# The first norm's weight row: spread by a broadcast transfer, or by TensorE into PSUM

## The reference, cut to what matters

```python
def _rmsnorm(x, g):
    y = x * lax.rsqrt(jnp.mean(x * x, axis=-1, keepdims=True) + NORM_EPS)
    return y * g

h = _rmsnorm(x, lw['g_pre_mix'])      # g_pre_mix: 1024 numbers, one for each column
z = h @ lw['w_in']                    # 1024 x 3488, column groups for the branches
```

## Time and profile before

| what | us |
| --- | --- |
| three executions | 906.77, 908.28, 906.37 |
| median | 906.77 |
| the profiled execution, its own time | 906.51 |
| its span (first to last instruction) | 904.7 |
| TensorE busy in the span | 884.0 |
| VectorE, ScalarE, GpSimd busy | 485.6, 389.0, 75.8 |

### The profile page before, as it was taken

The page is one execution under the profiler, slowest core; times in us unless marked ns, Lnnn a source line. Parts: engine busy times, 40 slices in busy tenths (PEclk is TensorE's granted clock), DMA queues, the critical chain, the costliest instruction groups (busy, mean ns, idle before and its releaser), DMA issues.

```text
span 904.7 us, 13767 instructions
## 1 busy us (share of the span) xinstructions
PE 884.0 (98%) x5501; PEld 802.5 (89%) x5501; DVE 485.6 (54%) x745; ACT 389.0 (43%) x772; POOL 75.8 (8%) x73
## 2 busy tenths in 40 slices
PE   8999999999999988999999999999999999999997
PEld 7888999999976767998789999999999998888885
DVE  5522533334354455564679877777777774343124
ACT  5211422344453565452666454544454443332112
POOL 0300297230030000000000000000000000000000
PEclk9999999999999999999999999999999999999999
DMA  7623245253230001654512333322233326222202
GB/s 270 183 72 91 77 129 169 70 145 104 86 70 1 2 1 40 200 181 175 198 71 70 93 94 95 93 78 78 80 93 94 93 83 242 72 74 90 70 23 117
DMA packets 101455, 91.97 MB, mean 102 GB/s; under 512 B 8480, under 2 KB 85296, under 8 KB 101248
## 3 DMA queue, kind: packets, MB, share of 16 engines
q1 hardware_dynamic: 95216, 86.45, 30.7%
q10 hardware_dynamic: 5280, 2.72, 1.1%
q0 software_dynamic: 896, 1.92, 0.7%
HBM read 79.60 MB, written 12.40 MB: 102 GB/s over the span
## 4 chain that ended last, share of the span: by engine, by line
PE 90%; DVE 5%; ACT 3%; DMA 1%; issue 1%; SPq 0%; ACTq 0%; DVEq 0%
PE ps L1153 26%; PE ps L1155 26%; PE ps L1154 26%; PE ps L1333 2%; PE ps L1382 1%; PE ps L1344 1%; PE ps L1429 1%; PE ps L1303 1%; PE ps L1376 1%; PE ps L1307 1%; DVE nm_c L1706 1%; ACT probs L875 1%; PE ps L1404 1%; PE ps L1414 1%; DMA raw<-in_w_in 1%
## 5 line engine op out<-in xcount | busy, mean ns | idle before, releaser
L1642 DVE TENSOR_TENSOR wlo<-raw,whi 128x1024 fp32r<-128x1024 f32 x59 | 78.8, 1338 | 204.6 <-ACT whi L802 197.1
L802 ACT ACTIVATE whi<-raw 128x1024 fp32r<-128x1024 f32 x59 | 62.1, 1057 | 179.8 <-PE ps L1155 177.8
L1153 PE MATMUL ps<-h_hi,wlo 128*128 128x320 f32 x288 | 90.7, 315 | 0.0
L1155 PE MATMUL ps<-h_hi,whi 128*128 128x320 f32 x288 | 88.9, 309 | 0.0
L1154 PE MATMUL ps<-h_lo,whi 128*128 128x320 f32 x288 | 88.9, 309 | 0.0
L1153 PE MATMUL ps<-sc_hi,t_lo 128*128 128x320 f32 x252 | 77.9, 309 | 1.7 <-DVE t_lo L1892 1.7
L1155 PE MATMUL ps<-sc_hi,t_hi 128*128 128x320 f32 x252 | 77.8, 309 | 0.0
L1154 PE MATMUL ps<-sc_lo,t_hi 128*128 128x320 f32 x252 | 77.8, 309 | 0.0
L1054 ACT ACTIVATE t_hi<-wd 128x512 fp32r<-128x512 f32 x84 | 52.8, 629 | 58.1 <-DVE wd L1905 53.7
L1153 PE MATMUL ps<-whi,gu_lo 128*128 128x512 f32 x190 | 74.0, 390 | 0.2 <-DVE gu_lo L1977 0.2
L1155 PE MATMUL ps<-whi,gu_hi 128*128 128x512 f32 x190 | 73.9, 389 | 0.0
(11 more groups left out here) (305 smaller groups left out, 2139.2 us busy)
## 6 DMA issues: line engine op xcount, KB each, us to landing
raw<-in_w_gate_up SPq DMA_DIRECT2D x44, 512.0 KB, 3.8
raw<-in_w_down SPq DMA_DIRECT2D x22, 512.0 KB, 3.7
raw<-in_w_in SPq DMA_DIRECT2D x16, 512.0 KB, 4.0
raw<-in_w_in SPq DMA_DIRECT2D x12, 480.0 KB, 5.2
gates_scratch<-gate_s SPq DMA_DIRECT2D x16, 320.0 KB, 2.4
gate_r<-gates_scratch SPq DMA_DIRECT2D x8, 640.0 KB, 4.1
raw<-in_w_branch SPq DMA_DIRECT2D x8, 512.0 KB, 5.1
raw<-in_w_out SPq DMA_DIRECT2D x8, 512.0 KB, 5.9
```

The lines of the kernel that those rows point to most:

```text
L802: act.activation(whi[:, r % 2, :] if to is None else to, raw[:, r, :], ACT.Copy).then_inc(w_hi, 1)
L1153: pe.matmul(out, left[1], right[0], start=first, stop=False, skip_group_check=not own_group)
L1155: return pe.matmul(out, left[0], right[0], start=False, stop=last, skip_group_check=not own_group)
L1642: dve.tensor_tensor(lo[:, place, :], raw[:, r, :], hi[:, place, :].bitcast(F32), ALU.subtract).then_inc(w_lo, 1)
```

## The change

The weight row is loaded as one row of 4 KB, by the first instruction of ScalarE's list. VectorE sets a row of 128 ones. TensorE multiplies the column of ones by the row, in two products of 512 columns with a contraction of one, into banks 3 and 4, which leaves the row in every partition of PSUM. VectorE's `h_scale` takes it from there for tiles 0 to 2. The broadcast transfer remains, but behind tile 3 in SyncE's queue, and serves tiles 3 and 4. The 44 turns ahead of `h_turn(0)` become 10 ahead of the two products, 18 behind them, and 12 behind `h_turn(0)`, all into bank 2.

```diff
+    gpre_1 = area("gpre_1", [1, D], 28704)
+    ones_1 = area("ones_1", [1, P], 29728)
...
             load_x(0)
-            sp.dma_start(gpre_b[:], g_pre_mix.to_broadcast([P, D])).then_inc(gpre_in, 16)
             for j in range(2):
                 load(j, win_v[:, 2 * j:2 * j + 2, 0:IN_CHUNK], IN_CHUNK)
                 load_x(j + 1)
-            for t in range(3, TILES):
-                load_x(t)
+            load_x(3)
+            sp.dma_start(gpre_b[:], g_pre_mix.to_broadcast([P, D])).then_inc(gpre_in, 16)
+            load_x(4)
...
         @block.scalar
         def _(act):
+            act.dma_start(gpre_1[:], g_pre_mix).then_inc(row_in, 16)
...
             pe.wait_ge(const_rdy, 1)
-            for n in range(44):
-                pe.transpose(ps[:, 7, 0:P], ident[:], ident[:])
+            def turn_identity(count):
+                for n in range(count):
+                    pe.transpose(ps[:, 2, 0:P], ident[:], ident[:])
+
+            turn_identity(10)
+            pe.wait_ge(ones_rdy, 1)
+            pe.wait_ge(row_in, 16)
+            for half in range(2):
+                ins = pe.matmul(ps[:, 3 + half, :], ones_1[0:1, :], gpre_1[0:1, 512 * half:512 * half + 512],
+                                start=True, stop=True)
+            ins.then_inc(gain_mm, 1)
+            turn_identity(18)
             h_turn(0)
+            turn_identity(12)
...
+            dve.memset(ones_1[:], 1.0).then_inc(ones_rdy, 1)
+
             def h_scale(t):
                 dve.wait_ge(h_sd, t + 1)
                 dve.reciprocal(r_h[:, t:t + 1], sd_h[:, t:t + 1]).then_inc(h_rs, 1)
                 dve.wait_ge(h_rs, t + 1)
-                dve.scalar_tensor_tensor(out=x_t[:, t, :], in0=x_t[:, t, :], scalar=r_h[:, t:t + 1], in1=gpre_b[:],
+                if t < 3:
+                    dve.wait_ge(gain_mm, 1)
+                    gain = ps[:, 3:5, :].rearrange("p b n -> p (b n)")
+                else:
+                    dve.wait_ge(gpre_in, 16)
+                    gain = gpre_b[:]
+                dve.scalar_tensor_tensor(out=x_t[:, t, :], in0=x_t[:, t, :], scalar=r_h[:, t:t + 1], in1=gain,
                                          op0=ALU.mult, op1=ALU.mult).then_inc(h_norm, 1)
 
-            dve.wait_ge(gpre_in, 16)
             h_scale(0)
```

More of the change, by code:

```diff
@@ L445, in build_layer @@
         h_ssq, h_sd, h_rs, h_norm, h_tr, h_hi_rdy, h_lo_rdy = (sem(n) for n in ("h_ssq", "h_sd", "h_rs", "h_norm", "h_tr", "h_hi_rdy", "h_lo_rdy"))
-        table_rdy = sem("table_rdy")
+        table_rdy, ones_rdy, gain_mm, row_in = (sem(n) for n in ("table_rdy", "ones_rdy", "gain_mm", "row_in"))
         bank_empty = sem("bank_empty")
```

## The result

The changed kernel takes 910.44 us (median of six executions, 909.48 to 910.75) where the kernel before takes 906.51 (905.87 to 908.28, six executions beside it). The ratio is 1.0039, 95% interval 1.0029 to 1.0049: slower by 0.4%, where 905.1 with a range from 904.4 to 907.2 was forecast.

The account below looks back on a forecast made before the run. The prediction took the start, in the first 28 us, to decide when a fixed block of TensorE work can begin. An earlier start (0.71) and the clock (0.91) give 1.62 us off 906.51; forecast 905.1, range 904.4 to 907.2.

Parts of the forecast that it names:

- Two float32 products take 3.70 / 8 = 0.46 each: TensorE's two new products of 512 columns: 0.46 us each at full pace, 0.92 at half.
- TensorE doubled its pace after 2.9 us of work, at about 4.5: First turns on TensorE: 13 of 44 at the slow pace, 0.217 us each, the others at 0.108.
- half to twice the price: Allowance for the two products, as contraction of one was not in the rows: 0.9 to 1.8 us in all.
- The eighteen turns: Turns on TensorE between products and tile 0's transposes: 0.108 us each, 1.94 in all, ending between 7.0 and 7.4.
- the root at 5.8: Root for tile 0, ahead of its scaling on VectorE: ready at 5.78 us.
- the ten turns: Turns on TensorE ahead of the products: 0.217 us each from 1.58, ending at 3.75.
- the row's landing: ScalarE's transfer of the weight row: issued at 0.75 us, landing between 3.15 and 4.25, taken as 3.7.
- B: Rival: pace doubles later, the eighteen turns delay tile 0's transposes by 0.8 us and eat the gain; 906.6, chance 0.15.
- Rival C: Pace not doubled before tile 0's transposes, which start at 10.0 us; 907.9 to 910.4, taken as 909.2, chance 0.08.
- block 0: First weight block in SyncE's queue: lands between 5.5 and 6.5 us instead of 7.72.
- the chain of 4.23 a tile: Copy to h_hi, statistics, scaling and transposes of the next tile: 4.23 us a tile, setting the pace up to tile 4.
- The gain of 0.91 from the clock: First to second copy to h_hi: twelve turns bridge TensorE's pause, the clock stays up, 0.91 us saved.

Follow-up runs that it names:

- e2: Changed kernel with 18 turns ahead of the two products and 10 behind, instead of 10 and 18: 909.51 us against 906.68, ratio 1.0032.
- e4: Changed kernel with no turns ahead of the two products and 28 behind: 909.01 us against 906.68 for the kernel before, ratio 1.0023.
- e1: Changed kernel with the two products on the 128-row identity instead of one-row operands, same columns and waits: 906.61 us against 906.68, ratio 0.9998.
- e9: Kernel before with 66 turns instead of 44 ahead of tile 0, nothing else: 908.13 us against 906.7, ratio 1.0018.
- e3: Kernel before with only twelve turns added behind the transposes of tile 0: 906.75 us against 906.68, ratio 0.9999.
- e5: Kernel before with 36 turns instead of 44 and twelve turns behind tile 0's transposes: 905.61 us against 906.28, ratio 0.9993.
- e8: e1 with 4 turns instead of 18 behind the full-height products: 905.96 us against 906.28 for the kernel before, ratio 0.9992.
- e6: Changed kernel with 2 turns instead of 18 behind the two products: 908.73 us against 906.28 for the kernel before, ratio 1.0026.
- e7: Kernel before with 10 turns, two unused one-row products from the identity and 18 turns replacing the 44 turns: 910.24 us against 906.28, ratio 1.0033.
- e10: Changed kernel once more, nothing edited, for a second profile: one execution, 909.25 us.

## Why the prediction was wrong

The forecast was 905.1, faster by 0.18%; the kernel is slower by 0.4%. By its own steps, of which the second is the one that cost the time:

**"Two float32 products take 3.70 / 8 = 0.46 each" is the first failed step, and a misreading of the earlier trace rows.** Near 254 us eight instructions stand in the timeline; but at this line the kernel asks for eight products in all (four jobs, two halves of the contraction), and the list by shape of the kernel before has sixteen instructions for them:

```profile
L1303 PE MATMUL ps<-ckv_T,w_uk 128*128 128x512 f32 x16 | 7.4, 605 | 0.0
```

A float32 product of 512 columns is two passes of 0.46. The two products are four passes: 1.98 at full pace (e2), 3.75 to 3.78 at half (e4, the changed kernel), 3.45 where the pace doubled during the last (e1). The bound of "half to twice the price" was drawn around the wrong figure and did not hold it.

**"TensorE doubled its pace after 2.9 us of work, at about 4.5" is the second, and the costly one.** It was read from one execution and carried over to a list with other work in it; that one-row products raise the clock like turns was taken for granted, without a row that shows it. Read from the weight loads one by one, the profiles without one-row products have it at 4.4 and 4.8 (the kernel before, e9) or at 6.5 to 7.05 (e1, e3, e5, e8). With one-row products ahead of it, it came at 11.6 to 12.6 (the changed kernel, e4, e6, e7, e10). The changed kernel and e1 differ in the operands of the two products alone, and in 3.8 us; that the identity's many zeros are not the reason shows e7, whose one row is taken from the identity too. Of the 5.3 us between forecast and result e1 gives back 3.8. The other 1.5 were not taken apart; in e1 the pace still doubles at 7.05 and not at 4.5, and four passes stand where two were counted.

**The eighteen turns** were put at 1.94 and took 3.70; the transposes of tile 0 were forecast at 7.36, measured at 11.29; the first copy at 8.05, measured at 12.23.

**Right were:** the root at 5.8 (5.76); the ten turns, forecast to end at 3.75 and over at 3.57; the row's landing, forecast at 3.7 and measured at 3.35 (e4), 2.6 behind its issue and so not held back to the landing of tile 0, as was argued in favour of B and C; the scaling with an operand from PSUM, 1.28 as before; block 0 a little better than the range of 5.5 to 6.5, at 5.4; the broadcast behind tile 3, for which nobody waited; the chain of 4.23 a tile; that what is lost at the second copy is lost at the end (e9); and that the twelve turns keep the clock up, in this kernel too (first copy 3.47 late, second 2.56). The fixed cost of about 2.0 us that the prediction takes from the Trainium skill ("DMA: Bandwidth & Descriptors", anatomy of one DMA) is given there for transfers issued by GpSimd; this row, issued by ScalarE, took 2.6.

**Rival C** named the place, TensorE's list ahead of the transposes at half pace, and its prices: 907.9 to 910.4, of which I took 909.2. It had a chance of 0.08, and its place was the right one. I held against it that in the rows the pace doubled after 2.9 us of turns. What I held for it, a late row and a wait ahead of the products, was not the cause: the row was there in time and TensorE did not stand still. So C had the place by its mechanism and not by its reason. The rows had nothing on products of one row, the new kind of work, and the sum gave them a price but no place among the things that raise the clock. The start cost 2.5 to 2.9 us, as C's mechanism says; the other 1.4 of the profiled execution, in the attention stage, was in no rival, and that the result lies near C's upper price of 910.4 is chance: C reaches it by a start 3.9 late.

**The gain of 0.91 from the clock** rested on the pause of 9.2 to 10.7. e3 shows that it is not to be had by the bridge alone: where the pace doubles late, the pause is not there, but the turns end late by the same amount. The step itself was read rightly: where neither stands in the way, in e5, the second copy is 4.22 behind the first, not 5.14, and 0.88 earlier than before. That the median gained by it is not shown.

## What to carry to other kernels

Work that is to raise TensorE's clock should look like the work it stands in for: instructions on all 128 rows. Two products of one row by 512 columns left the clock where it was: low in the changed kernel, where they kept the engine busy for 3.8 us in the profile, and high in e2, where they took 1.98. Only the heights 1 and 128 were tried, so where between them it changes is open. Filler in a list that is taken in order is safe only if it ends in time at the slow pace as well; and how many instructions one product is stands in the count of the list by shape.

## What was not expected of the hardware

TensorE was busy without a gap from 1.58 to 11.7 us and was at its lower clock all the time, because 3.7 us of it went to one-row products (e1 against the changed kernel: 7.05 against 11.7). The Trainium skill ("TensorE: Matmul & The Clock Gate", Part 1) says that a monitor sets the clock by how busy the engine has been; these runs agree only if busy does not mean the profile's busy time.

The time at which the pace first doubles differs between profiles of almost the same start: from 4.4 to 7.0 with turns alone from 1.58 on (the kernel before 4.4, e9 4.8, e5 6.5, e3 7.0). One profile can't give it.

With the clock up before them, the four one-row passes took 1.98 us and did not lower it in that time (e2).
